# One core, two-layer encoder: in the second attention the transposes move ahead of the value products, both results get a second buffer, and finished head pairs are read back early into the input of the output projection

## The reference, cut to what matters

```
def _swa_sinks(h, w_q, sinks, w_o, k_band, v_band):
    q = (h @ w_q).reshape(B, nc, CHUNK, KV_B, GROUP_B, HEAD_DIM)
    s = jnp.einsum('bnqgrd,bnkgd->bngrqk', q, k_band).astype(jnp.float32) / math.sqrt(HEAD_DIM)
    s = s - slopes * dist                      # a bias table, chunk against two chunks
    ...
    m = jnp.maximum(jnp.max(s, axis=-1, keepdims=True), sink)
    e = jnp.exp(s - m)
    denom = jnp.sum(e, axis=-1, keepdims=True) + jnp.exp(sink - m)
    p = (e / denom).astype(v_band.dtype)
    o = jnp.einsum('bngrqk,bnkgd->bnqgrd', p, v_band).reshape(B, S, H_B * HEAD_DIM)
    return o @ w_o
```

## Time and profile before

| what | value |
|---|---|
| three timed runs, median (lowest, highest) | 2517.85 us (2514.11, 2519.14) |
| the profiled execution: device time, span | 2521.02 us, 2519.2 us |
| granted TensorE clock, mean over the span | 0.966 |
| TensorE busy, share of the span | 2337.5 us, 93% |
| VectorE, ScalarE, GpSimd busy | 61%, 46%, 47% |

### The profile page before, as it was taken

One profiled execution on the slowest core, in us unless ns is written; L12 is line 12 of the kernel. 1 busy time (PEld: TensorE's weight loads), 2 busy tenths in 40 slices (PEclk: granted clock), 3 DMA queues, 4 the chain that ended last, 5 costly groups with the idle time before them and its releaser, 6 DMA issues.

```text
span 2519.2 us, 30443 instructions
## 1 busy us (share of the span) xinstructions
PE 2337.5 (93%) x10984; PEld 1932.2 (77%) x10984; DVE 1536.2 (61%) x2470; ACT 1149.7 (46%) x1933; POOL 1172.5 (47%) x1580
## 2 busy tenths in 40 slices
PE   4899999997989999999999898988899999999996
PEld 3778788886867777777778687776678888888884
DVE  4565656557777666666664766773375555444456
ACT  4365665748044333333333566662354333333334
POOL 3411313120646666666666351204356666666660
PEclk9989999999999999999999899978899999999998
DMA  6111211113821333333331321114111111111111
GB/s 259 52 47 34 68 34 54 47 47 102 316 76 58 117 118 114 122 121 118 118 105 57 111 68 40 51 34 175 42 34 51 51 51 51 63 55 52 58 51 67
DMA packets 66007, 206.91 MB, mean 82 GB/s; under 512 B 7345, under 2 KB 7985, under 8 KB 65730
## 3 DMA queue, kind: packets, MB, share of 16 engines
q1 hardware_dynamic: 29760, 109.06, 13.2%
q10 hardware_dynamic: 36098, 95.91, 11.6%
HBM read 186.66 MB, written 16.32 MB: 81 GB/s over the span
## 4 chain that ended last, share of the span: by engine, by line
PE 65%; DVE 14%; ACT 8%; POOL 4%; issue 4%; DMA 4%; ACTq 1%; DVEq 0%; POOLq 0%
PE bank L883 38%; PE bank L620 17%; POOL w_spl L549 2%; DVE X L1889 2%; PE bank L636 1%; POOL w_raw L556 1%; DVE H L1610 1%; PE bank L780 1%; PE bank L754 1%; PE bank L815 1%; PE bank L790 1%; POOL S3f L556 1%; PE bank L816 1%; PE bank L817 1%; DVE cV L1859 1%
## 5 line engine op out<-in xcount | busy, mean ns | idle before, releaser
L883 PE MATMUL bank<-H,w_spl 128*128 128x512 f32 x3744 | 880.6, 393 | 33.3 <-DVE H L1610 14.6
L883 PEld LDWEIGHTS bank<-H,w_spl 128*128 128x128 f32 x3744 | 704.3, 189 | 198.0 <-DVE X L1889 29.4
L549 POOL TENSOR_TENSOR w_spl<-w_raw,w_spl 128x256 fp32r<-128x256 f32 x688 | 544.9, 820 | 443.5 <-ACT w_spl L1358 442.1
L620 PE MATMUL bank<-H,w_spl 128*128 128x512 f32 x2016 | 520.7, 408 | 24.9 <-DVE H L1610 10.7
L883 PE MATMUL bank<-TB,w_spl 128*128 128x512 f32 x2112 | 492.5, 389 | 0.3 <-ACT sU L1373 0.3
L620 PEld LDWEIGHTS bank<-H,w_spl 128*128 128x128 f32 x2016 | 386.5, 197 | 106.4 <-issue 20.6
L883 PEld LDWEIGHTS bank<-TB,w_spl 128*128 128x128 f32 x2112 | 396.2, 188 | 83.4 <-issue 0.9
L1358 ACT ACTIVATE w_spl<-w_raw 128x512 fp32r<-128x512 f32 x328 | 201.9, 628 | 546.7 <-PE bank L883 332.9
L487 POOL TENSOR_TENSOR pace<-one_s 128x1 f32<-128x1 f32 x50 | 13.4, 267 | 737.6 <-PE bank L780 355.8
L1889 DVE SCALAR_TENSOR_TENSOR X<-bank,mods,X 128x1024 f32<-128x1024 f32 x176 | 225.0, 1279 | 34.2 <-PE bank L883 34.2
L1882 DVE TENSOR_TENSOR bank<-bank,sU 128x512 f32<-128x512 f32 x80 | 55.9, 699 | 299.7 <-PE bank L883 299.7
(11 more groups left out here) (171 smaller groups left out, 3186.5 us busy)
## 6 DMA issues: line engine op xcount, KB each, us to landing
w_raw<-in_w_stream SPq DMA_DIRECT2D x184, 512.0 KB, 3.8
ada_raw_f<-in_ada_t ACTq DMA_DIRECT2D x128, 256.0 KB, 2.9
ada_raw_o<-in_ada_t ACTq DMA_DIRECT2D x8, 2048.0 KB, 8.3
ada_raw<-in_ada_t SPq DMA_DIRECT2D x8, 1024.0 KB, 18.6
negF<-scratch_f ACTq DMA_DIRECT2D x16, 512.0 KB, 3.8
X<-in_x_t SPq DMA_DIRECT2D x4, 1024.0 KB, 10.8
X<-in_x_t ACTq DMA_DIRECT2D x4, 1024.0 KB, 8.1
scratch_x<-X ACTq DMA_DIRECT2D x1, 4096.0 KB, 12.6
```

Source lines behind the costliest of these rows:

```text
L549: last = pool.tensor_tensor(block_at(layer, b, 1, q, q + 256), src[:, q:q + 256], block_at(layer, b, 0, q, q + 256).bitcast(F32), ALU.subt ...
L620: last = pe.matmul(dst, stat(k, a), mov(k, b), start=(k == 0 and a + b == 0), stop=(k == KT - 1 and a == 1))
L883: last = pe.matmul(dst, block_at(layer, b, x, k * P, k * P + P), mov(y), start=(start and x + y == 0), stop=(stop and x == 1), skip_group_ ...
```

## The change

Four things change. (1) On TensorE `turn_b(u - 2)` comes ahead of `values_b(u - 3)`; DVE does the maxima first, then `q_low`, then the low part into `PTB`, and the normalisation and the addition last; the addition is that of unit u - 3 and no longer u - 4; ACT does `O_tmpB` ahead of the exponentials. (2) `PTB` and `O_stB` are two buffers each; an addition that begins a head pair waits for the transfers of the pair before the last. (3) `O_raw` is gone: a head pair is read back straight into the place of its low part in `H` (`Hf` is the same memory as f32), pairs 0 to 6 inside the loop from u = 27 on, and ACT and DVE make the parts of pairs 0 and 1 inside it too (`PAIR_LOADS`, `PAIR_SPLITS`). `X` is read back ahead of the last high part. (4) The output projection begins with k = 0 to 6 of tile 0, then k = 0 to 6 of tile 1, then k = 7 of both. In the second layer tiles 0, 2, ... use banks 6 and 7, tiles 1, 3, ... banks 4 and 5.

```
+PAIR_LOADS = {27: (0, 1, 2), 28: (3, 4), 30: (5,), 33: (6,)}
+PAIR_SPLITS = {33: (0,), 34: (1,)}
+PAIRS_BEHIND = list(range(2, 8))
+OUT_BEHIND = list(range(7))
...
+        Hf = at("Hf", [P, KT, 2, S], F32, 0)
-        PTB = at("PTB", [P, 2, 512], F32R, 182)
+        PTB = [at(f"PTB{i}", [P, 2, 512], F32R, kb) for i, kb in enumerate((182, 200))]
-        O_stB = at("O_stB", [P, S], F32, 190)
+        O_stB = [at(f"O_stB{i}", [P, S], F32, kb) for i, kb in enumerate((190, 204))]
...
+            def out_first(ks):
+                for k in ks:
+                    if k == 0:
+                        pe.wait_ge(w_ready, tile_order(W_OUT_B) + 1)
+                        pe.wait_ge(qB_lo, 16)
+                    pe.wait_ge(o_lo, 8 + k + 1)
+                    out_step(1, 0, k, int(k == 0))
+            def out_two():
+                out_first(OUT_BEHIND)
+                pe.wait_ge(w_ready, tile_order(W_OUT_B + 1) + 1)
+                pe.wait_ge(o_addB, 64)
+                for k in range(KT - 1):
+                    out_step(1, 1, k)
+                out_first([KT - 1])
+                out_step(1, 1, KT - 1, 1)
...
+                if 2 <= u <= 33:
+                    turn_b(u - 2)
                 if u >= 3:
                     values_b(u - 3)
-                if 2 <= u <= 33:
-                    turn_b(u - 2)
...
+            def load_pair(k):
+                if k == 0:
+                    act.wait_ge(qB_ps, 16)
+                for e in range(2):
+                    act.wait_ge(o_outB[k % 2][e], 16 * (k // 2 + 1))
+                act.dma_start(Hf[:, k, 1], dO[k]).then_inc(ob_in[k], 16)
+            def pair_high(k):
+                act.wait_ge(ob_in[k], 16)
+                nc.scalar.activation(H[:, k, 0], Hf[:, k, 1], ACT.Copy).then_inc(o_hi, 1)
...
             send_pair(7)
-            out_proj()
+            for k in PAIRS_BEHIND[:-1][:2]:
+                pair_high(k)
+            load_pair(7)
+            for k in PAIRS_BEHIND[2:-1]:
+                pair_high(k)
+            for j in range(4):
+                act.dma_start(X[:, 2 * j:2 * j + 2], dX.rearrange("k p s -> p k s")[
+                    :, 2 * j:2 * j + 2]).then_inc(x_in[j], 16)
+            pair_high(7)
...
+            def pair_low(k):
+                dve.wait_ge(o_hi, 8 + k + 1)
+                V_.tensor_tensor(H[:, k, 1], Hf[:, k, 1], H[:, k, 0].bitcast(F32), ALU.subtract).then_inc(o_lo, 1)
...
-                    if v % 4 == 0 and v:
+                    if v % 4 == 0 and v >= 8:
                         for e in range(2):
-                            dve.wait_ge(o_out[e], O_OUT_A + 16 * (v // 4))
+                            dve.wait_ge(o_outB[v // 4 % 2][e], 16 * (v // 8))
```

More of the change, by code:

```diff
@@ L211, in program @@
         O_rawA = at("O_rawA", [P, 4, S], F32, 128)
-        O_raw = at("O_raw", [P, 4, S], F32, 168)
         wvg = at("wvg", [P, KT, 2, 272], F32R, 128)
@@ L356, in program @@
         o_in = [sem(f"o_in{i}") for i in range(4)]
+        o_outB = [[sem(f"o_outB{i}{e}") for e in range(2)] for i in range(2)]
+        ob_in = [sem(f"ob_in{k}") for k in range(KT)]
         o_hi = sem("o_hi")
@@ L973, in ffn @@
                 return used[0]
-            out_proj(0)
+            for m in range(8):
+                out_tile(0, m)
             square_sum(1, 1)
@@ L1052, in values_b @@
                     for part in range(2):
-                        last = pe.matmul(bank(4 + u % 2, j * P, j * P + P), v, PTB[:, part, j * P:j * P + P],
+                        last = pe.matmul(bank(4 + u % 2, j * P, j * P + P), v, PTB[u % 2][:, part, j * P:j * P + P],
                                          start=(part == 0), stop=(part == 1))
@@ L1069, in _ @@
                     pe.wait_ge(vs_in, 48)
+                if 2 <= u <= 33:
+                    turn_b(u - 2)
                 if u >= 3:
                     values_b(u - 3)
-                if 2 <= u <= 33:
-                    turn_b(u - 2)
                 if u < 27:
                     q_quarter((u + 1) // 4 + 1, (u + 1) % 4)
-            out_proj(1)
+            out_two()
+            for m in range(2, 8):
+                out_tile(1, m)
             square_sum(3, 1)
@@ L1307, in _ @@
                 load_ada(m + 2)
[L1309 to L1328, removed]
             def ffn(layer):
@@ L1820, in out_proj @@
                 gc = M_G1 + M_L1 * layer
-                for k in range(8 if layer else 0):
-                    dve.wait_ge(o_hi, 8 * layer + k + 1)
-                    V_.tensor_tensor(H[:, k, 1], O_raw[:, k % 4], H[:, k, 0].bitcast(F32),
-                                     ALU.subtract).then_inc(o_lo, 1)
                 for m in range(8):
@@ L1994, in _ @@
             dve.wait_ge(vs_in, 48)
-            for u in range(36):
-                if u <= 27 and u % 2:
-                    q_low(u // 4 + 1, u % 4 // 2)
+            def pair_low(k):
+                dve.wait_ge(o_hi, 8 + k + 1)
+                V_.tensor_tensor(H[:, k, 1], Hf[:, k, 1], H[:, k, 0].bitcast(F32), ALU.subtract).then_inc(o_lo, 1)
+            for u in range(35):
                 if u < 32:
@@ L2015, in _ @@
                     V_.tensor_scalar(nmB[:, b], mxB[:, b], sink_s[:, hp:hp + 1], -1.0, ALU.max, ALU.mult).then_inc(mB, 1)
+                if u <= 27 and u % 2:
+                    q_low(u // 4 + 1, u % 4 // 2)
+                if 2 <= u <= 33:
+                    v = u - 2
+                    dve.wait_ge(ptB_hi, v + 1)
+                    V_.tensor_tensor(PTB[v % 2][:, 1], bank(2 + v % 2), PTB[v % 2][:, 0].bitcast(F32),
+                                     ALU.subtract).then_inc(ptB_lo, 1)
                 if 1 <= u <= 32:
```

80 lines of the change are left out of this document (43 added, 37 removed).

## The result

| | median of the timed runs | lowest, highest |
|---|---|---|
| before | 2516.36 us | 2514.11, 2519.14 |
| after | 2478.64 us | 2476.55, 2479.91 |

The account below looks back on a forecast made before the run. TensorE, busy for 93% of the span, was taken as the bound, through its waits and slow-clock stretches. Gains of 34.8 us, less 1 us, took 2521.02 to 2487.0; timed runs' median lies 3.2 us lower: 2484 us, range 2476 to 2498.

Parts of the forecast that it names:

- predicted signs: Profile after: 4.96 us iterations, no value-product waits, 26 to 27 us for units 28 to 34, near 186 us to tile 2.
- Part 1: Iterations with query products, unit 3's to unit 28's scores (stretch A): TensorE's waits vanish, 143.75 to 122.5 us, 21.2 us less.
- Part 2: Units 28 to 34 (stretch B), clock staying at half: 31.64 to 26.5 us, 5.1 us less, read-backs charged nothing.
- Part 3: Seam before the output projection: first product waits 1.8 us instead of 10.51, 8.7 us less, later pairs covered.
- Part 4: First two output tiles: same 96 matmuls, tile 2 waits for tile 0's addition, 0.2 us more.
- The sum: Whole change: 21.2 + 5.1 + 8.7 - 0.2 = 34.8 us gained, 1 us taken off for handings over.
- A: The forecast itself, whole kernel: 2484 us, own range 2479 to 2489, chance 0.64.
- B: Rival in the query iterations: clock still falls once per head pair, keeping 7.9 us; 2492 us, chance 0.12.
- C: Rival at the seam: partly open, pairs 2 to 7, `X` or weight tile 3 late by 3-8 us; about 2490, chance 0.08.
- D: Rival: units 28 to 34 at full clock, 3.3 us there and up to 2.4 in part 4; 2479 us, chance 0.10.
- E: Rival: lead given back later because POOL's weight blocks may hold the FFN; 2518 us, chance 0.03.
- F: Rival: slower, small matmuls in one block keep the clock at half in query iterations; some 2573 us, chance 0.03.

Follow-up runs that it names:

- e8: Changed kernel plus two multiplications with unread results on VectorE ahead of the low part in `PTB`, in six iterations; one execution took 2500.03 us.
- e1: Kernel before with only VectorE's order changed, the maxima ahead of `q_low`; timed 15.5 us faster than before, ratio 0.9917 to 0.9957.
- e2: Kernel before with only TensorE's order changed, transposes ahead of value products; timed 11.3 us faster than before, ratio 0.9937 to 0.9972.
- e6: Changed kernel with a single `PTB`; timed 30.0 us faster than the kernel before, ratio 0.9864 to 0.9901.
- e7: Changed kernel with output tiles 0 and 1 in plain order; timed 38.7 us faster than the kernel before, ratio 0.9834 to 0.9868.
- e9: Changed kernel with high parts of pairs 0-5, low parts of 0-3 (on POOL) and tile 0's k = 0-3 inside units 29 to 34; 2474.07 us.
- e4: Kernel before (old orders, single buffers) with early reading back, early splits and interleaved output tiles; timed 1.0 us faster, ratio 0.9986 to 1.001.
- e11: Kernel before with early reading back, early splits, interleaved output tiles and two `O_stB`; timed 6.7 us faster, ratio 0.9953 to 0.998.

## Why the prediction was right, point by point

**The mechanism, a low part that costs as a wait and as a clock: right.** e8 shows both parts, and e1 and e2 show that either order lifts the clock. The predicted signs are in the profile but for two: iterations of 4.93 and 5.03 us, 4.96 in the mean, no wait at the value products, clock 1.00, the landing gone from VectorE's waits, and 186.5 us for "near 186". The two: in the wait ahead of the first output product 1.52 us stand for 2, and TensorE's wait stands at the transposes of the last units, twice (0.82 and 1.42 us), where the prediction had one pass of the last unit, 2.7 us, that "cannot be covered"; the sum of these with the 1.52 us is 3.8 us.

**Part 1**, -21.2 us: measured -21.1. The timetable, of which the text gives only the outcome, said what the orders and buffers give together, and the sum came out. It did not say which edit gives what, and the runs say that the second `PTB` gives nothing here.

**Part 2**, -5.1 us: measured -5.2. It hangs on the second `PTB`: without it B is 33.73 us (e6). The charge of nothing for seven read-backs was 0.3 us too low.

**Part 3**, -8.7 us: measured -9.0. Pair 7 was given "some 14 us" behind the last value products and is subtracted 13.8 us behind them. The cover of "14 steps of k" for it was not needed here (e7), though without it 0.4 us are left.

**Part 4**, +0.2 us: from the first output product to the addition of tile 2 it is 35.9 us, and it was 35.1 us: +0.7. The clock is back 3 us behind the first output product, and it was nearly 5 us before, so the excess is not the clock's. What failed is part 3's "it keeps ahead from pair 2 on". VectorE's subtractions were to take 1.23 to 1.3 us each; the last four take 6.32 us together, 1.58 us each, and TensorE's weight loads wait for them at k = 2, 4, 5 and 6 of tile 0, up to 0.46 us each. POOL kept up: no wait for a weight tile is listed. Timeline of VectorE and of the weight loads, after:

```profile
1679.53 6.32 DVE L2032 TENSOR_TENSOR H<-Hf,H 128x1024 fp32r<-128x1024 f32 x4 [0.39 <-ACT H L1554]
...
1682.55 1.22 PEld L629 LDWEIGHTS bank<-H,w_spl 128*128 128x128 f32 x6 [0.45 <-DVE H L2032]
1684.22 5.77 PEld L629 LDWEIGHTS bank<-H,w_spl 128*128 128x128 f32 x26 [0.46 <-DVE H L2032]
```

**The sum**, 34.8 us: the stage shows 34.6. The 1 us taken off for handings over was not there; this is the mis-sized term, with part 4's 0.5 us against it. (2521.02 - 34.8 + 1 is 2487.2, not 2487.0; the forecast stays 2484.) Timed, the gain is 37.7 us, and 3.1 us of it lie outside the stage. The median, 2478.64 us, is therefore 5 us under the forecast and just under A's own range of 2479 to 2489. The last matmul of the value projection, ahead of this attention and in code that no version touched, starts anywhere between 1480.7 and 1487.2 us in the fourteen profiles, so executions differ by that much. Between the two profiled executions 3.5 us are there already at that point. The uncertainty of the ratio, about 4 us, holds such a difference. The forecast also stood against the median of three runs, which moved by 1.5 us with a fourth.

**The rivals.** B fell: the mean clock is 1.00 over all 25 iterations. Its reason, the 20 small matmuls that stay, did not matter without the idle time; e8 shows drops with that block and an idle time behind four of six. C fell with e7 and the timeline: nothing near 3 us is left open. D fell: units 28 to 34 stay at 0.50 with TensorE busy for 24.19 of 26.44 us. The rule of the Trainium skill, TensorE: Matmul & The Clock Gate, Part 1, that "activity releases the throttle" would have put the time at 2479; the timed median is near that figure, but not for that reason, since the stretch on which the rule bears took 26.44 us at half clock, where D had 3.3 us less. E fell: the lead of the stage reaches the end. F fell with the clock of 1.00 in stretch A.

## What to carry to other kernels

Ask of each operand that the busiest engine waits for what stands ahead of it in its producer's queue. Here two exchanges of order, with nothing added, gave half of the gain. A second buffer is worth what the order behind it leaves exposed: the same `O_stB` was worth 6.3 us with one order and nothing with the other, the same `PTB` 7.3, 1.9 or 0 us, by the stretch and the order around it. Parts that remove the same wait don't add, and an early transfer can be paid for by another transfer on its queue; so test a change with several parts both ways, alone on the old kernel and taken out of the new one.

## What the hardware showed that was not expected

Six idle times of TensorE of 1.69 or 1.70 us were followed by half clock in four cases and by full clock in two; so a wait of this length has two prices, and the mean of many is what counts.

In units 28 to 34 of the changed kernel TensorE is busy for 24.19 of 26.44 us, with matmuls of 128 columns, and the clock stays at 0.50. In e9, where six products of 512 columns stand among them, it is 0.59 in the 5 us in which they run and 1.00 in the next 5 us. The Trainium skill's sentence on activity, named above, fits the second and not the first. What in e9 made the difference was not isolated.

A transfer of 256 KB that lands in 3.0 to 3.4 us in the changed kernel landed in 7.0 to 7.5 us when it was issued behind three reads of 512 KB on the same queue (e4, e11).
